# A merge product over the tokens in parts of 512, 512 and 80 columns, in place of three parts of 368

## The reference

```python
x = x + 0.5 * swiglu(rmsnorm(x, n_f1), f1_g, f1_u, f1_d)
h = rmsnorm(x, n_mix);  proj = h @ w_in          # mixer A: short conv, mixer B: gated delta rule
merged = sigmoid(gate_a) * (y_a @ w_a) + sigmoid(gate_b) * (y_b @ w_b)
x = x + merged @ w_o
x = x + 0.5 * swiglu(rmsnorm(x, n_f2), f2_g, f2_u, f2_d)
```

## Time and profile before

| | |
|---|---|
| runs | 3450.96, 3452.89, 3457.15 us, median 3452.89 |
| the profiled execution, span | 3453.9 us (the page gives no time beside the span) |
| TensorE busy | 3322.5 us, 96% of the span |
| VectorE, ScalarE, GpSimd busy | 38%, 29%, 26% |
| mean granted TensorE clock | 0.975 |
| last product of the merge, TensorE | 2513.5 to 2613.1 us |

### The profile page before, as it was taken

One profiled execution on the slowest core, in us unless ns is written; L12 is line 12 of the kernel. 1 busy time (PEld: TensorE's weight loads), 2 busy tenths in 40 slices (PEclk: granted clock), 3 DMA queues, 4 the chain that ended last, 5 costly groups with the idle time before them and its releaser, 6 DMA issues. The chain is left out here.

```text
span 3453.9 us, 51790 instructions
## 1 busy us (share of the span) xinstructions
PE 3322.5 (96%) x20286; PEld 3236.0 (94%) x20286; DVE 1326.3 (38%) x2186; ACT 1013.5 (29%) x1408; POOL 891.1 (26%) x506
## 2 busy tenths in 40 slices
PE   8999999998999799999999999879999999999998
PEld 8999999998999699899999998769999999999998
DVE  4333333334777433333333333333223333333333
ACT  5111111114222354444444454321024111111113
POOL 2121121214122333323333333212233121111112
PEclk9999999999999899999999999779999999999998
DMA  4111111112222212112112121354312111111111
GB/s 135 40 49 43 43 43 43 43 43 79 73 86 88 81 51 69 58 51 68 58 51 75 51 69 36 99 195 151 120 38 74 43 43 49 43 43 43 36 30 52
DMA packets 274431, 222.74 MB, mean 64 GB/s; under 512 B 12042, under 2 KB 251786, under 8 KB 274288
## 3 DMA queue, kind: packets, MB, share of 16 engines
q1 hardware_dynamic: 273988, 220.56, 21.0%
q10 hardware_dynamic: 324, 0.41, 0.0%
HBM read 170.66 MB, written 50.28 MB: 64 GB/s over the span
## 5 line engine op out<-in xcount | busy, mean ns | idle before, releaser
L209 PE MATMUL ffn_bank<-ffn_h_hi,ffn_w_hi 128*128 128x368 f32 x2112 | 698.2, 331 | 6.8 <-DVE ffn_h_lo L618 6.8
L210 PE MATMUL ffn_bank<-ffn_h_lo,ffn_w_hi 128*128 128x368 f32 x2112 | 699.2, 331 | 0.0
L211 PE MATMUL ffn_bank<-ffn_h_hi,ffn_w_lo 128*128 128x368 f32 x2112 | 697.9, 330 | 0.0
L209 PE MATMUL mix_bank<-mix_h_hi,mix_w_hi 128*128 128x368 f32 x1752 | 639.5, 365 | 6.6 <-DVE mix_pre L1750 3.2
L408 POOL TENSOR_TENSOR ffn_w_lo<-g_w_raw,ffn_w_hi 128x1024 fp32r<-128x1024 f32 x130 | 310.9, 2400 | 1191.4 <-ACT ffn_w_hi L404 1191.3
L210 PE MATMUL mix_bank<-mix_h_lo,mix_w_hi 128*128 128x368 f32 x1752 | 580.3, 331 | 0.0
L211 PE MATMUL mix_bank<-mix_h_hi,mix_w_lo 128*128 128x368 f32 x1752 | 579.0, 330 | 0.0
L209 PEld LDWEIGHTS ffn_bank<-ffn_h_hi,ffn_w_hi 128*128 128x128 f32 x2112 | 398.3, 189 | 8.1 <-issue 8.0
L211 PEld LDWEIGHTS ffn_bank<-ffn_h_hi,ffn_w_lo 128*128 128x128 f32 x2112 | 398.0, 188 | 0.0
L210 PEld LDWEIGHTS ffn_bank<-ffn_h_lo,ffn_w_hi 128*128 128x128 f32 x2112 | 397.8, 188 | 0.1
L817 POOL TENSOR_TENSOR mix_w_lo<-g_w_raw,mix_w_hi 128x1024 fp32r<-128x1024 f32 x73 | 186.0, 2549 | 782.0 <-ACT mix_w_hi L812 782.0
(11 more groups left out here) (242 smaller groups left out, 4559.5 us busy)
## 6 DMA issues: line engine op xcount, KB each, us to landing
g_w_raw<-in_w_in SPq DMA_DIRECT2D x73, 512.0 KB, 6.0
g_w_raw<-in_ffn_w_gate SPq DMA_DIRECT2D x44, 512.0 KB, 3.8
g_w_raw<-in_ffn_w_up SPq DMA_DIRECT2D x44, 512.0 KB, 3.8
g_w_raw<-in_ffn_w_down SPq DMA_DIRECT2D x44, 512.0 KB, 3.5
scratch_qkv<-mix_out SPq DMA_DIRECT2D x24, 552.0 KB, 2.8
turn_kq<-scratch_qkv SPq DMA_DIRECT2D x32, 256.0 KB, 3.9
scratch_x<-g_x SPq DMA_DIRECT2D x8, 552.0 KB, 7.2
scratch_z<-turn_z_out SPq DMA_DIRECT2D x8, 552.0 KB, 2.8
```

What stands on the lines that cost most here:

```text
L209: pe.matmul(out, w_hi, x_hi, start=first, stop=False)
L210: pe.matmul(out, w_hi, x_lo, start=False, stop=False)
L211: return pe.matmul(out, w_lo, x_hi, start=False, stop=last)
```

## The change

For r = 2 alone the tokens are cut as columns 0 to 511, 512 to 1023 and 1024 to 1103 (`full_bank`), on TensorE, in VectorE's addition to x, in ScalarE's squares and in GpSimd's sums. The first two products (r = 0 and 1) keep the parts of 368, and so do both SwiGLUs. Numbers of instructions, semaphores, banks and loop orders stay as they are. `square_part` and `add_part`, which the SwiGLU uses, are not changed.

```diff
+def full_bank(b):
+    return slice(512 * b, min(512 * (b + 1), T))
...
-    def __init__(self, s, rstd, sq):
-        self.rstd, self.sq = rstd, sq
+    def __init__(self, s, rstd, sq, part=third):
+        self.rstd, self.sq, self.part = rstd, sq, part
...
-        act.activation(self.sq[:, third(n % NB)], x_part, ACT.Square).then_inc(self.squared, 1)
+        act.activation(self.sq[:, self.part(n % NB)], x_part, ACT.Square).then_inc(self.squared, 1)
...
-        part = third(n % NB)
+        part = self.part(n % NB)
         pool.tensor_tensor(self.rstd[:, part], self.rstd[:, part], self.sq[:, part], ALU.add).then_inc(self.added, 1)
...
-        nrm = NextNorm(s, rstd, y_raw[:, 0, :])
+        nrm = NextNorm(s, rstd, y_raw[:, 0, :], full_bank)
...
-            def product(j, b, k):
-                return three_passes(pe, bank[3 * j + b][:, 0:TH], w.hi[:, j, k, :], w.lo[:, j, k, :],
-                                    y_hi[:, k, third(b)], y_lo[:, k, third(b)], k == 0, k == KC - 1)
+            def product(r, j, b, k):
+                part = (full_bank if r == 2 else third)(b)
+                return three_passes(pe, bank[3 * j + b][:, 0:part.stop - part.start], w.hi[:, j, k, :], w.lo[:, j, k, :],
+                                    y_hi[:, k, part], y_lo[:, k, part], k == 0, k == KC - 1)
...
-                    nrm.square(act, x[:, bass.ds(i * 2 + (2 * ahead + j), 1), third(b)].rearrange("p o t -> p (o t)"), i, 6, n)
+                    nrm.square(act, x[:, bass.ds(i * 2 + (2 * ahead + j), 1), full_bank(b)].rearrange("p o t -> p (o t)"), i, 6, n)
...
-                            ps = bank[3 * j + b][:, 0:TH]
+                            part = (full_bank if r == 2 else third)(b)
+                            ps = bank[3 * j + b][:, 0:part.stop - part.start]
...
-                            xc = x[:, bass.ds(i * 2 + j, 1), third(b)].rearrange("p o t -> p (o t)")
+                            xc = x[:, bass.ds(i * 2 + j, 1), part].rearrange("p o t -> p (o t)")
```

More of the change, by code:

```diff
@@ L2060, in weight_block @@
                     for k in range(KC):
-                        mm = product(j, b, k)
+                        mm = product(r, j, b, k)
                     mm.then_inc(unit_done, 1)
@@ L2077, in _ @@
                     for b in range(NB):
-                        mm = product(0, b, k)
+                        mm = product(r, 0, b, k)
                         if k == KC - 1:
```

## The result

Five runs of the changed kernel took 3466.80 to 3476.07 us, median 3470.27, against 3452.89 before: the ratio is 1.0046, with a 95% interval from 1.0034 to 1.0059, some +12 to +20 us. The same kernel run again on another occasion gave 3470.49 against 3454.72 (1.0040, 1.0026 to 1.0054). It is slower, and clear of noise.

What follows compares the result with a forecast made beforehand. TensorE was taken to bound the last product. Product +14.5 us and end -1.2 give +13.3: 3467.2 by the span, 3466 on the timed footing; own range 3459 to 3469 (chance 0.61), all together 3457 to 3475.

Steps and rivals of the forecast that it cites:

- What bounds the kernel: Last product: TensorE is busy without a gap, so it lasts as long as its 576 matmuls follow one another.
- The 512-column matmul, 233 ns: Last product: cost grows with columns from 167.5 ns at 368, giving 233 ns; 214 and 228 kept for the range.
- The 13.5 ns that only the full clock shows: Last product: part of a 368-column matmul's 167.5 ns beyond the 154 ns scaled from half clock.
- The bound of 214: Last product: lower bound in ns for a 512-column matmul, half-clock pace at double the clock; +7.2 us for the product.
- the fixed part (228): Last product: 512-column matmul at 228 ns if 13.5 ns are fixed for each matmul; +12.6 us for the product.
- The 80-column matmul, 112 ns: Last product: too short to hide the 128-column weight load, so 112 ns instead of 36 ns by columns.
- The sum of the product, +14.5 us: Last product: 192 triples (three matmuls, one chunk and pass over all tokens) go from 502.6 to 578 ns each.
- VectorE, ScalarE and GpSimd in the loop at nothing: Last product's blocks: their work, GpSimd's the most at 5.3 us a block, lies under TensorE and costs nothing.
- No wait is added: Last product's loop: the change adds no wait between engines and moves no DMA; size nothing.
- second rival: Last product: clock falls in narrow stretches, 1.7 us each; every block 3478, two or three 3470; chance 0.09.
- The end, -1.2 us: Behind the merge's last matmul: VectorE, ScalarE and GpSimd handle 80 columns; -1.2 us, bounds -1.2 and 0.
- Rivals one, three and four: Last product: plain float32 rate, 3471, 0.15; fixed cost with cheap load, 3453, 0.11; only columns left, 3444, 0.04.

Runs made afterwards that it cites:

- chunks outside: Changed kernel with the last product's eight blocks all looping over chunks outside and the three parts inside, so narrow matmuls come three at a time: 3470.34 us, 1.0041.
- narrow part first: Changed kernel with the last product's parts ordered as 80, 512 and 512 columns: 3471.83 us, 1.0042 of the kernel before.
- splits first: Changed kernel with GpSimd splitting both weight blocks of a loop turn before adding the squares: 3464.99 us, 1.0031 of the kernel before.

## Why the prediction was right

**What bounds the kernel.** Right: every change of a matmul's price went into the time, and behind the product's start the only engine that kept TensorE waiting in the kernel after was GpSimd, once, for 0.4 us.

**The 512-column matmul, 233 ns.** Right: the starts are 233 ns apart in the median. The 13.5 ns that only the full clock shows do grow with the columns: 256, 368, 424, 464 and 512 columns take 118, 168, 193, 211 and 233 ns in the median, 0.46 ns a column throughout; a straight line through the five leaves some 3 ns to a fixed part, as an estimate, not 13.5. The bound of 214 and the fixed part (228) are out. One support of the forecast was none: the eight plain float32 matmuls of 128 columns in the earlier trace rows each load 128 weight columns as well, so their 111 ns are the load's pace, and "four times the columns, 3.9 times the distance" says nothing of a fixed part.

**The 80-column matmul, 112 ns.** Right in size and in cause. That it is the next matmul's weight load was argued from 16-column matmuls of the mixer; the 16 columns in place of 80 (same price) and the 64 weight columns in place of 128 (half the price) show it, and so do the loads in the kernel after, which keep the pace of 111 ns from the start of a run while the first narrow matmul does not.

**The sum of the product, +14.5 us.** Right within a tenth: a regular block gives 575.4 - 503.3 = 72.1 ns a triple, +13.8 us for 192; the forecast had 75.5, because 502.6 was 0.7 low and a wide matmul takes 232 ns in the mean, if the narrow run is counted at 24 x 111.7 ns = 2.68 us of the block. The first block grew by 1.55 us only. Without wait and fall the product is 112.5 us (three profiles, 112.47 to 112.73), +13.4.

**VectorE, ScalarE and GpSimd in the loop at nothing.** Wrong by one term. I summed GpSimd's work in a block (5.3 of 13.8 us) and didn't follow the order in which it comes: one split waits behind three sums. "No wait is added" is the step that failed: the wait cost 0.4 us, and the clock fell behind it. The sign stood in the earlier trace rows: before the change TensorE's weight load had already waited 0.2 us for that low part.

**The clock, second rival at 0.09 for a fall in several blocks.** A granted clock below 1.00 inside the product was named as a sign of being wrong, and it came: the clock fell, once in the last product, with wait and fall together some 2.0 us (114.60 and 114.72 against 112.54), of which some 1.7 are the fall, the price that the rival gave. So this rival took part in the result, though it is not what carries it. The mechanism put forward, narrow matmuls alone, isn't what the runs show at 80 columns: with all three products so cut, fourteen narrow runs of the first two and six of seven in the third kept their clock. A run of 24 and then a start 0.4 us late lost it, in all three profiles of 80 columns that had both; in the three profiles without the late start (chunks outside, narrow part first, splits first) it stayed. But 176 columns, also 112 ns a matmul, kept it through a start 0.7 us late, and 16 columns lost it without one. What sets the fall off stays open.

**The end, -1.2 us.** Right: 2.59 became 1.40.

**The forecast as a whole.** By terms it is 15.4 - 1.2 = +14.2 us in the profiles, against +13.3 forecast: 1.1 us less for the triple, 2.0 us more for wait and clock, two errors that partly cancel. Timed it was +17.4 and, in the second comparison, +15.8, both with the interval around 14.2. The medians of 3470.27 and 3470.49 lie above the forecast's own range of 3459 to 3469 and inside the range of all together, near the 3470 of the second rival with two or three falls and the 3471 of the first; the traces, not the time, tell them from the forecast. The two profiled spans differ by 20.4 us, but 7.2 of these lie before the merge (its first matmul starts at 2313.18 in place of 2305.94, and at 2309.53 in the second profile of the same kernel), where nothing is changed; over the ten other profiles that start lies anywhere between 2303.41 and 2309.53. One execution isn't enough to read a few us from a span; the touched stretch is. That I took the page's span for the whole time was wrong by the 1.8 us around it; the difference is the same on either footing.

**Rivals one, three and four** are out by the 112 ns of 80 and of 16 columns: no fall to the rate of plain float32, no cheaper load, nothing faster.

## What to carry to other kernels

Where each matmul brings its own weights, a part narrower than the load's time has a price that doesn't shrink: here 112 ns for 128 weight columns, so by an estimate a cut loses below about 112/0.456 = 246 float32r columns; of the cuts tried, 176 columns lost time and 256 did not. Before filling banks with 512 columns, look what is left for the last part. An engine with time to spare can still be late for one block if its queue holds other work first; follow the order, not the sum. A wait of 0.2 us in the rows before can be the sign that there is no slack.

## What the runs showed of the hardware

- Float32r at full clock goes at 0.455 to 0.461 ns a column from 256 to 512 columns, with a fixed part of some 3 ns by a straight line through the five widths, while half clock gives 0.837, less than twice as much.
- The weight load as a floor is 112 ns for 128 columns and 58 to 59 ns for 64 at full clock.
- TensorE's clock fell where a start came 0.4 us late behind 2.6 us of 80-column matmuls, while starts 0.7 us late (behind 176 columns), 0.8 us (behind 256) and 1.6 us (behind 80 columns at 58 ns) at the same place left it at 1.00. Why the run behind the second block lost it with 16 columns and not with 80 was not tried further.
